# First stage: one VectorE instruction per convolution tap, and step 3's weight transposes two slots later

## What is computed

```python
h  = rms_norm(x)
z  = h @ w_in                      # 2048 -> GLU-a | GLU-b | q | k | v | gate_conv | gate_attn
# convolution branch: prompt and sample are two sequences, each with its own 30 frames of history
glu = z_a * sigmoid(z_b)
u   = concatenate([history, glu])  # history: zeros for the prompt, state_conv for the sample
c   = depthwise_conv(u, width=31) + bias      # then LayerNorm, swish, w_conv_out
# attention branch, 8 heads; the prompt is masked to chunks of 64, the sample sees 256 past frames + itself
p = softmax(q k^T / 8)             # twice per head: p1, p2
o = (p1 - lambda * p2) @ v         # then a norm per head, w_attn_out
```

## Time and profile before

| | us |
|---|---|
| median of three executions | 3962.49 |
| the three executions | 3959.23, 3962.49, 3965.61 |
| span of the profiled execution (first to last instruction) | 3965.6 |
| PE busy | 3818.9 (96%) |
| DVE busy | 3049.1 (77%) |
| ACT busy | 1099.4 (28%) |
| POOL busy | 1318.5 (33%) |

### The profile page before, as it was taken

How to read it: one execution, slowest core, us unless ns; L and a number is a source line. 1 busy time by engine, 2 the same in 40 slices (tenths; PEclk the granted TensorE clock), 3 DMA queues, 4 the chain that set the end, 5 groups by cost and what they waited for, 6 DMA issues and landing times.

```text
span 3965.6 us, 67094 instructions
## 1 busy us (share of the span) xinstructions
PE 3818.9 (96%) x24995; PEld 3757.7 (95%) x24995; DVE 3049.1 (77%) x3858; ACT 1099.4 (28%) x1126; POOL 1318.5 (33%) x923
## 2 busy tenths in 40 slices
PE   8999999999989998999999999999999999999999
PEld 7989999999889998999999999999999999999999
DVE  6887888788855445388859999998678888888876
ACT  3323233232222112222233333332222222222222
POOL 3333333333334342454532222222133323333320
PEclk9999999999999999999999999999999999999999
DMA  7789888887878998799979999999888989888895
GB/s 275 262 313 325 289 281 299 320 301 265 308 260 284 319 380 308 264 372 369 353 251 385 387 383 383 389 379 390 314 313 340 353 321 343 342 329 337 338 350 189
DMA packets 451684, 1285.17 MB, mean 324 GB/s; under 512 B 34368, under 2 KB 258368, under 8 KB 343360
## 3 DMA queue, kind: packets, MB, share of 16 engines
q1 hardware_dynamic: 372576, 876.99, 62.1%
q0 software_dynamic: 46080, 335.56, 21.5%
q10 hardware_dynamic: 32832, 70.07, 4.6%
HBM read 1070.18 MB, written 345.75 MB: 357 GB/s over the span
## 4 chain that ended last, share of the span: by engine, by line
PE 42%; issue 32%; POOL 14%; DMA 7%; DVE 3%; ACT 1%; POOLq 0%; SPq 0%; DVEq 0%; ACTq 0%
PE ST L1951 19%; PE ST L1859 17%; POOL w_lo L654 14%; DMA w_raw<-w_all 4%; PE PA L1859 3%; PE ST L1927 2%; DMA rows<-v_rows,v_idx 2%; DVE w_lo L1009 1%; ACT w_hi L717 1%; DVE PA L1518 1%; DMA rows<-u_rows,v_idx 1%; PE PA L1841 1%; PE ST L1874 0%; DMA u_rows<-u_out 0%; POOL w_lo L646 0%
## 5 line engine op out<-in xcount | busy, mean ns | idle before, releaser
L654 POOL TENSOR_TENSOR w_lo<-w_raw,w_hi 128x512 fp32r<-128x512 f32 x588 | 793.3, 1381 | 1218.1 <-ACT w_hi L717 1184.6
L717 ACT ACTIVATE w_hi<-w_raw 128x2048 fp32r<-128x2048 f32 x368 | 703.7, 1913 | 1334.5 <-PE ST L1951 513.2
L1951 PE MATMUL ST<-wt_hi,w_hi 128*128 128x384 f32 x2048 | 686.5, 335 | 13.9 <-DVE w_lo L1009 13.7
L1951 PE MATMUL ST<-wt_hi,w_lo 128*128 128x384 f32 x2048 | 684.5, 334 | 0.0
L1951 PE MATMUL ST<-wt_lo,w_hi 128*128 128x384 f32 x2048 | 684.3, 334 | 0.0
L1009 DVE TENSOR_TENSOR w_lo<-w_raw,w_hi 128x2048 fp32r<-128x2048 f32 x219 | 501.1, 2288 | 206.5 <-ACT w_hi L717 199.2
L690 POOL DMA_INDIRECT rows<-v_rows,v_idx x160 | 323.2, 2020 | 736.0 <-DVE PA L1518 667.0
L1619 PE MATMUL PA<-h_hi,w_hi 128*128 128x272 f32 x2496 | 541.1, 298 | 3.8 <-DVE w_lo L1009 3.8
L1619 PE MATMUL PA<-h_hi,w_lo 128*128 128x272 f32 x2496 | 521.7, 291 | 0.0
L1619 PE MATMUL PA<-h_lo,w_hi 128*128 128x272 f32 x2496 | 520.2, 290 | 0.0
L1859 PE MATMUL ST<-h_hi,w_hi 128*128 128x384 f32 x1408 | 508.8, 361 | 2.2 <-ACT h_b L917 1.6
(11 more groups left out here) (272 smaller groups left out, 6241.9 us busy)
## 6 DMA issues: line engine op xcount, KB each, us to landing
w_raw<-w_all SPq DMA_DIRECT2D x368, 1024.0 KB, 7.5
u_in<-w_all SPq DMA_DIRECT2D x128, 1024.0 KB, 8.6
u_rows<-u_out SPq DMA_DIRECT2D x512, 256.0 KB, 7.4
v_rows<-w_all SPq DMA_DIRECT2D x128, 1024.0 KB, 10.3
a_scr<-gb ACTq DMA_DIRECT2D x128, 192.0 KB, 6.3
g_scr<-g_st ACTq DMA_DIRECT2D x24, 1024.0 KB, 11.3
gl_st<-g_scr SPq DMA_DIRECT2D x30, 768.0 KB, 10.6
a_st<-a_scr SPq DMA_DIRECT2D x30, 768.0 KB, 13.2
```

The lines of the kernel that those rows point to most:

```text
L654: ins = pool.tensor_tensor(w_lo[:, slot, cols], raw[:, slot, cols], w_hi[:, slot, cols].bitcast(F32), ALU.subtract)
L717: act.activation(w_hi[:, slot, :], raw[:, slot, :], ACT.Copy).then_inc(hi_ready, 1)
L1951: last = mm(PB[n % 2][:, k, :], a, r_[b][:, c, :], start=(c == 0 and y == 0), stop=(c == GRP - 1 and y == 2))
```

## The change

There are two parts.

*Taps.* One instruction covers the 574 columns from w to w + 573 of `u` (512 prompt, 30 that belong to the history gap and give values that nobody reads, 32 sample). It adds up in a buffer of its own, `c_run`, of 574 columns; `xg` is no longer used for it, and so ACT's wait for `conv_done` before it writes `xg` goes. `c_tp` and `c_ts` go, and the two stores of the result read `c_run[:, 0:512]` and `c_run[:, 542:]`. The wait for the previous head's stores (`c_stored`) moves from the last tap to the first. `a_t` moves to where `c_tp` was.

*Step 3.* On PE `weights_t` and `mix_values` of step 3 stand two slots later: (7, 1) and (7, 2) in place of (6, 3) and (7, 0). On ACT the copy `att_at` of step 3 stands behind `z_slot` of unit 6 in place of ahead of it, and `att_o` of step 3 behind `att_exp` of step 4 in place of ahead of it.

```diff
@@ ACT, z_slot
                 if i in (0, 1):
                     act.wait_ge(norm_done, m + 1)
-                    act.wait_ge(conv_done, h + 1)
...
@@ ACT, the loop over units of a head (s = i - 3)
-                        if s > 0:
+                        if s > 0 and s != QT:
                             att_o(h, g - 1, s - 1)
                         if 0 <= s < STEPS:
                             att_exp(g, s)
                             if s == 0:
                                 values_out(h)
-                            att_at(g, s)
+                            if s == QT:
+                                att_o(h, g - 1, s - 1)
+                            if s != QT - 1:
+                                att_at(g, s)
...
                         z_slot(hp, r, i)
+                        if s == QT - 1:
+                            att_at(g, s)
@@ DVE, taps
-                    segs = ((0, TP, 0), (TP, T, HIST))
+                    src = u[:, w:w + TP + HIST + TS]
                     if w == 0:
                         dve.wait_ge(glu_ready, h + 1)
+                        dve.wait_ge(c_stored, h * 32 + 1)
+                        own.by(V.tensor_scalar(c_run[:, :], src, cw, par[:, bass.ds(h + P_CB, 1)], ALU.mult, ALU.add))
                     else:
                         settle()
-                    for a, b, sh in segs:
-                        src = u[:, a + sh + w:b + sh + w]
-                        if w == 0:
-                            own.by(V.tensor_scalar(xg[:, a:b], src, cw, par[:, bass.ds(h + P_CB, 1)], ALU.mult, ALU.add))
-                        elif w < TAPS - 1:
-                            own.by(V.scalar_tensor_tensor(xg[:, a:b], src, cw, xg[:, a:b], ALU.mult, ALU.add))
...
+                        ins = V.scalar_tensor_tensor(c_run[:, :], src, cw, c_run[:, :], ALU.mult, ALU.add)
+                        (own.by(ins) if w < TAPS - 1 else ins.then_inc(conv_done, 1))
@@ PE, head_hooks
-                    for d, f in ((0, scores), (3, weights_t), (4, mix_values)):
+                    late = 2 if s == QT - 1 else 0
+                    for d, f in ((0, scores), (3 + late, weights_t), (4 + late, mix_values)):
```

More of the change, by code:

```diff
@@ L165, in build @@
         u_out = ar.take("u_out", [P, 2, UNITW])
-        c_tp = ar.take("c_tp", [P, TP])
+        a_t = ar.take("a_t", [P, TP])
         az = Area(MT, MEND - MT)
@@ L172, in build @@
         e = az.take("e", [P, 2, TP])
-        a_t = az.take("a_t", [P, TP])
         u = az.take("u", [P, HIST + TP + HIST + TS])
         rs1 = az.take("rs1", [P, T])
-        c_ts = az.take("c_ts", [P, TS])
+        c_run = az.take("c_run", [P, TP + HIST + TS])
         xs = Area(Y0, HALF).take("xs", [P, KD, T])
@@ L760, in z_slot @@
                     act.wait_ge(conv_done, h + 2)
-                    act.dma_start(c_scr[bass.ds(h, 1), :, 0:TP].rearrange("a p n -> p (a n)"), c_tp[:, :]).then_inc(c_stored, 16)
-                    act.dma_start(c_scr[bass.ds(h, 1), :, TP:T].rearrange("a p n -> p (a n)"), c_ts[:, :]).then_inc(c_stored, 16)
+                    act.dma_start(c_scr[bass.ds(h, 1), :, 0:TP].rearrange("a p n -> p (a n)"), c_run[:, 0:TP]).then_inc(c_stored, 16)
+                    act.dma_start(c_scr[bass.ds(h, 1), :, TP:T].rearrange("a p n -> p (a n)"), c_run[:, TP + HIST:]).then_inc(c_stored, 16)
                     act.wait_ge(norm_done, h * 3 + 4)
@@ L1144, in o_norm @@
                                        ohi.bitcast(F32), ALU.mult, ALU.subtract).then_inc(norm_done, 1)
-            per_head = 2 * 6 + 4 * STEPS + QT + 1 + (2 * TAPS - 1) + 3
+            per_head = 2 * 6 + 4 * STEPS + QT + 1 + (TAPS - 1) + 3
             with dve.Fori(0, NH // 2) as hp:
```

## The result

The changed kernel takes 3908.93 us (median of 4 executions, 3907.31 to 3910.94) against 3962.31 us before (4 executions, 3959.23 to 3965.61). The ratio is 0.9864, 95% interval 0.9852 to 0.9876: 53.4 us less, where 34 were forecast and 3912 was the low end of the range. The span of its profiled execution is 3908.5 us.

A forecast was written before the change was run, and what follows sets the result against it. DVE's time until step 4's mix was taken to bound each head: 1.7 us of tap work plus 2.3 of waits, 8 x 4.0 = 32, plus 2 between heads, 34 us off, median 3928 us; 8-in-10 range 3912 to 3954.

The forecast's parts named there:

- What bounds the stage: First stage: DVE's time until step 4's mix sets PE's time; moving step 3's transposes buys nothing by itself.
- The taps, work: DVE's taps: merged instruction 0.82 us free, 0.96 apart; 1.7 us a head less work until step 4, 2.7 over all.
- The taps, waits for POOL: DVE's taps held by POOL's weight subtraction: 2.3 us a head less until step 4, bounded by -1 and 6.
- the walk: Following POOL's pieces against DVE's taps, instruction by instruction, in heads 1 and 2: 3.1 us less in head 1, 2.2 in head 2.
- Step 3, two slots later: PE and ACT: step 3's stall goes whole, mix_values has no wait, PE waits 0.6 to 0.9 us at step 4's transposes.
- The stall and the clock, from PE's side: PE without waits would reach step 4's transposes 4.9 us sooner in head 1, 4.6 in head 2, clock fall included.
- Between the heads of a pair: PE's wait on ACT's square at the change of heads: 0.5 us less each, 4 times, 2 us.
- Rival B: PE gets all it can, and the stall between heads ends with its clock fall: 44 us, 3918; chance 10%.
- The sum: Whole kernel: 32 us from the heads plus 2 between them, 34 us off; median 3928 us.
- A: Taps: only the work goes, the 82 us of waits for POOL stay; 11.6 us gain, 3951; chance 20%.
- C: Slower: ACT's copy for step 3 comes late behind z_slot 6, clock fall lies behind step 4; 3968 to 3974; chance 6%.
- D: No change: as C without clock falls, or the gain returns as longer waits for transfers, DMA share 0.92 wanted; chance 9%.

The follow-up runs named there:

- e2: Kernel before with only step 3's transposes, product and copy moved later on PE and ACT, taps still two instructions each: 3969.46 us, ratio 1.0026.
- e6: Kernel before with step 3's transposes and product two slots later on PE alone, ACT's copy where it was: 3966.94 us, ratio 1.0025.
- e1: Changed kernel with the old order on ACT and PE, so the merged taps alone: 3906.17 us, ratio 0.9864 to the kernel before.
- e4: Changed kernel with POOL filling most of w_lo with zeros in the first stage instead of subtracting: 3889.85 us, ratio 0.9821 to the kernel before.
- e3: Kernel before with POOL filling most of w_lo with zeros in the first stage instead of subtracting: 3888.76 us, ratio 0.9816.
- e5: Merged taps alone, but each tap split into two instructions of 287 columns: 3967.03 us, ratio 1.0023 to the kernel before.
- e11: Merged taps alone, POOL subtracting a unit in eight instructions of 128x256 instead of four of 128x512: 3899.63 us, ratio 0.9828 to the kernel before.
- e12: Merged taps alone, POOL subtracting a unit in two instructions of 128x1024 instead of four of 128x512: 3941.05 us, ratio 0.9936 to the kernel before.
- e7: Merged taps alone, with unit 0's evacuation and rotary step and unit 1's evacuation ahead of the turns between them: 3920.56 us, ratio 0.9913 to the kernel before.
- e10: Merged taps alone, with the rotary steps of units 0 and 1 each ahead of the turn behind its evacuation: 3931.70 us, ratio 0.9928 to the kernel before.
- e9: Merged taps alone, with only unit 0's rotary step exchanged with the turn behind its evacuation: 3924.12 us, ratio 0.9906 to the kernel before.

## Why the prediction was wrong, point by point

- **What bounds the stage: right.** The move alone gives nothing (e2, e6), the taps alone give all (e1). In e6 PE gained step 3's stall and waited 6.47 us at step 4 in place of 0.53.
- **The taps, work: right in kind, a little low.** Free 0.82 us, from the rows, was 0.821 in e4. Until step 4 the work gives 2.0 us (e4 beside e3, taps alone), not 1.7.
- **The taps, waits for POOL: the step that failed.** I bounded it by -1 and 6 us, walked it to 2.2 in head 2 and 3.1 in head 1, and took 2.3 for all. It is 3.9 in even heads and 2.4 to 2.7 in odd ones. So the walk was 0.4 us too high for head 1 (2.7) and 1.7 too low for head 2; that 2.3 comes near the odd heads is luck. Less the taps' work, the three groups of head 2 gave 0.9, 1.8 and 1.2 us, where I had said 1, about 1 and "about even"; those of head 1 gave 0.9, 1.5 and 0.3. The third group of head 2 was the largest error. DVE's timeline of head 2, from the four taps ahead of `evac` to step 4's maximum, before:

```profile
402.14 5.11 DVE L1125 SCALAR_TENSOR_TENSOR xg<-u,params_sb,xg 128x512 f32<-128x512 f32 x8
407.18 0.72 DVE L1052 TENSOR_TENSOR zb<-PA,rs 128x544 f32<-128x544 f32 x1
407.81 4.29 DVE L1125 SCALAR_TENSOR_TENSOR xg<-u,params_sb,xg 128x512 f32<-128x512 f32 x4
412.03 0.74 DVE L1083 TENSOR_REDUCE small<-ST 32x2 f32<-32x576 f32 x1
```

  After:

```profile
388.40 4.48 DVE L1125 SCALAR_TENSOR_TENSOR c_run<-u,params_sb,c_run 128x574 f32<-128x574 f32 x4
392.81 0.71 DVE L1055 TENSOR_TENSOR zb<-PA,rs 128x544 f32<-128x544 f32 x1
393.44 2.97 DVE L1125 SCALAR_TENSOR_TENSOR c_run<-u,params_sb,c_run 128x574 f32<-128x574 f32 x2
396.33 0.74 DVE L1086 TENSOR_REDUCE small<-ST 32x2 f32<-32x576 f32 x1
```

  9.89 us became 7.93, 1.96 less, of which six taps' work is 0.6; of the rest, 0.2 comes back on the small multiply behind the maximum (0.47 us, 0.16 before). POOL does start against the taps ahead of `evac` now, as I said, but it finds half as many instructions to hold there. I had weighed the bound of 6 us by the fear that the next long tap meets the next piece. e5 is that fear tested: with as many instructions as before the held time is as before, with half as many it is half. The Trainium skill (SBUF — State Buffer, Who interferes with whom) says that a VectorE instruction with two SBUF inputs and a GpSimd one that reads SBUF exclude each other. The runs agree, and e11 and e12 put numbers to it; what I drew from it, that it speaks against counting the short ones' waits, was the error.
- **Step 3, two slots later: right.** No wait at the transposes or at `mix_values`, POOL's third group sooner, and 1.15 us at step 4 in odd heads (0.6 to 0.9 forecast). The copy was in time only because the taps had become faster: with the old ones it is 5.26 us late (e2).
- **The stall and the clock, from PE's side: too low.** I gave PE 4.6 us in even heads; their PE length fell by 5.8 to 6.0. Head 2 had 3.7 us of idle time and has none now: besides step 3's 3.09 us I had left out a wait of 0.57 at an earlier step's transposes (of the 28.4 us of L1700, step 3 makes 23.6). The other 2.1 us of head 2 are busy time, where I had counted 1.5 for the clock. Over the stage busy time gave 19.4 us; at 1.5 us a head I had counted 12.
- **Between the heads of a pair: too low.** 0.5 us each. The wait on the square fell by 12.8 - 7.0 = 5.8 us in four places, 1.5 each, and with it goes some of the clock; from a head's first matmul to its DVE stretch the four odd heads became 6.1 us shorter in all, not 2. Rival B had 2.0 each there, and B as a whole, 44 us and 3918, came nearest.
- **The sum.** Four even heads gave 23.6 us where I counted 16. The odd ones gave 51.1 - 23.6 = 27.5, where I counted 18: 18.0 in the DVE stretches (16 counted), 6.1 ahead of them (2 counted) and some 3.5 behind them (none counted), 1.9 of which are the wait on `o_lo` at the end of the stage. All these errors have the same sign. The one that weighs most is in the even heads: I priced the waits for POOL low, although by my own count the short instructions alone waited about 4 us in head 1, and I took PE's ceiling from two stalls only.
- **Rivals.** A fell with e5 turned round: the held time does not stay when the count halves. C is real in its place, but for the kernel with the old taps: e2 is slower by 0.26%, and that by a longer DVE stretch and not by the clock fall that C had priced. D's worry on the transfers did not come: the DMA share of head 1 is 0.92, as computed, and e4 runs a head in 122.9 us with the same transfers. But the turns' stores do set the pace at the change of heads (e7 to e10).

Not settled: how much of the odd heads' remaining 4 to 7 us over 122.9 is the turns' transfers and how much the waits for POOL in the first units of a head. e3 and e4 had both turns and transfers and lost only 0 to 1.3 us there, which points to POOL; e7, e9 and e10 show that no exchange of turns tried here helps.

## What to carry to other kernels

Where VectorE works on two SBUF inputs beside GpSimd, count its instructions, not their columns: every one that meets a GpSimd instruction waits for that one's rest, so merge short instructions even where dead columns are computed, and cut GpSimd's instruction smaller. Where engines are taken out to measure waits, look for new idle time before taking the difference of two lengths: here it hid nearly half of the work that merging saves. Taking away a stall that another engine's time explains only moves it, and a clock fall that lay ahead of the old waiting point then costs its full price. For a term with wide bounds, test the walk on the kernel before: a walk that doesn't give back the waits that its own trace shows is no ground for taking the low value.

## What the runs showed of the hardware that I had not expected

- The held time of a VectorE tap fell from 1.71 to 0.75 to 0.31 us as GpSimd's instruction went from 1024 to 512 to 256 columns, with 49, 56 and 79 of 240 taps held; GpSimd's shortest such instructions took 2.37, 1.26 and 0.72 us. GpSimd paid for it: 440.6 us of busy time over the subtractions of 70 units in e11, 353.5 in e12.
- A 128x2 multiply on SBUF (L1089 after) takes 0.75 us on average, its namesake without POOL's reads in e4 0.22 us, though it reads two numbers a partition from a single tensor; in the kernel before it took 0.55 us. The transposes of `turn` (128x2048, from a single tensor too) are not lengthened: 2.30 us on average after, 2.31 in e4.
